# Attention stages of a fused two-block transformer kernel: the value products between a pair's two groups of transposes, the scores of a later pair behind them

## The reference, cut to what matters

```python
s = q @ k.T * scale + bias          # scores
p = exp(s - max(s)); p = p / sum(p) # softmax over the keys
o = p @ v                           # value products
```

## Time and profile before

| what | value |
|---|---|
| median of 3 runs | 3514.08 us |
| lowest, highest | 3511.32, 3519.0 us |
| profiled execution, its own time | 3510.07 us |
| its span | 3508.3 us |
| mean granted TensorE clock | 0.969 of full |
| busy, TensorE matmul | 3260.1 us (93%) |
| busy, VectorE | 2317.3 us (66%) |
| busy, ScalarE | 1332.2 us (38%) |
| busy, GpSimd | 1377.1 us (39%) |

### The profile page before, as it was taken

How to read it: one execution, slowest core, us unless ns; L and a number is a source line. 1 busy time by engine, 2 the same in 40 slices (tenths; PEclk the granted TensorE clock), 3 DMA queues, 4 the chain that set the end, 5 groups by cost and what they waited for, 6 DMA issues and landing times. The chain is left out here.

```text
span 3508.3 us, 51517 instructions
## 1 busy us (share of the span) xinstructions
PE 3260.1 (93%) x18667; PEld 2828.7 (81%) x18667; DVE 2317.3 (66%) x4682; ACT 1332.2 (38%) x2000; POOL 1377.1 (39%) x738
## 2 busy tenths in 40 slices
PE   7878999997999999999898889899989988899998
PEld 5756799997999999999686567788878866668877
DVE  7763989999996888887685667655450067654440
ACT  3344233334554433333312674322231145743331
POOL 3114347765765422222230564222223322444443
PEclk9988999999999999999999999999999999999999
DMA  6412547776999999998355503222212141033322
GB/s 208 153 39 78 186 138 253 233 226 209 365 369 356 359 366 362 367 358 309 126 174 136 92 2 128 82 60 63 62 45 63 47 124 59 33 130 92 94 79 89
DMA packets 235687, 588.98 MB, mean 168 GB/s; under 512 B 52547, under 2 KB 113987, under 8 KB 231404
## 3 DMA queue, kind: packets, MB, share of 16 engines
q1 hardware_dynamic: 177964, 419.63, 36.4%
q0 software_dynamic: 36864, 134.23, 10.5%
q10 hardware_dynamic: 20672, 32.68, 2.6%
HBM read 529.03 MB, written 56.91 MB: 167 GB/s over the span
## 5 line engine op out<-in xcount | busy, mean ns | idle before, releaser
L433 POOL TENSOR_TENSOR ahead_low<-w_raw,ahead_high 128x1024 fp32r<-128x1024 f32 (+1 forms) x159 | 422.0, 2654 | 891.3 <-ACT ahead_high L369 891.3
L230 PE MATMUL psum<-h_low,ahead_high 128*128 128x512 f32 (+1 forms) x1384 | 492.2, 356 | 0.0
L229 PE MATMUL psum<-h_high,ahead_high 128*128 128x512 f32 (+1 forms) x1384 | 491.3, 355 | 0.8 <-POOL ahead_low L433 0.8
L231 PE MATMUL psum<-h_high,ahead_low 128*128 128x512 f32 (+1 forms) x1384 | 489.3, 354 | 0.0
L369 ACT ACTIVATE ahead_high<-w_raw 128x1024 fp32r<-128x1024 f32 (+1 forms) x159 | 178.0, 1119 | 744.3 <-PE psum L231 710.0
L2075 POOL TENSOR_TENSOR pick_u_low<-pick_u_raw,pick_u_high 128x1024 fp32r<-128x1024 f32 x128 | 309.8, 2422 | 191.2 <-ACT pick_u_high L2194 188.9
L229 PE MATMUL psum<-peer_h_high,pick_u_high 128*128 128x384 f32 x1024 | 355.2, 347 | 15.6 <-POOL pick_u_low L2075 15.4
L230 PE MATMUL psum<-peer_h_low,pick_u_high 128*128 128x384 f32 x1024 | 348.4, 340 | 0.0
L231 PE MATMUL psum<-peer_h_high,pick_u_low 128*128 128x384 f32 x1024 | 345.3, 337 | 0.0
L229 PEld LDWEIGHTS psum<-h_high,ahead_high 128*128 128x128 f32 x1384 | 260.3, 188 | 43.3 <-issue 2.4
L231 PEld LDWEIGHTS psum<-h_high,ahead_low 128*128 128x128 f32 x1384 | 260.9, 188 | 38.7
(11 more groups left out here) (435 smaller groups left out, 8175.4 us busy)
## 6 DMA issues: line engine op xcount, KB each, us to landing
pick_u_raw<-in_expert_uT SPq DMA_DIRECT2D x128, 512.0 KB
v_raw<-in_expert_v SPq DMA_DIRECT2D x128, 512.0 KB
mod_w<-in_w_mod SPq DMA_DIRECT2D x88, 512.0 KB, 3.9
w_raw<-in_ffn_up SPq DMA_DIRECT2D x84, 512.0 KB, 3.6
gelu_dram<-pick_gelu ACTq DMA_DIRECT2D x128, 192.0 KB
gates_dram<-gate_plane SPq DMA_DIRECT2D x24, 1024.0 KB
g<-gates_dram SPq DMA_DIRECT2D x31, 768.0 KB
w_raw<-in_ffn_down SPq DMA_DIRECT2D x29, 704.0 KB, 4.1
```

The lines of the kernel that those rows point to most:

```text
L229: nc.tensor.matmul(bank, w_high, x_high, start=first, stop=False)
L230: nc.tensor.matmul(bank, w_high, x_low, start=False, stop=False)
L231: return nc.tensor.matmul(bank, w_low, x_high, start=False, stop=last)
L433: nc.gpsimd.tensor_tensor(w_low[r % 2][:, :, :], raw[r % n_raw][:, :, :], w_high[r % 2][:, :, :].bitcast(F32), ALU.subtract).then_inc(k.w_ ...
```

## The change

The order of the TensorE loop over the pairs is another one. Nothing is added or removed, and no other engine's program changes. For each w: lower transposes of w, value products of w-1, upper transposes of w, scores of w+2.

```diff
             for w in range(n):
                 turn(w, 0)
+                if w:
+                    multiply(w - 1)
+                turn(w, 1)
                 if w + 2 < n:
                     score(w + 2)
-                turn(w, 1)
-                if w:
-                    multiply(w - 1)
             multiply(n - 1)
```

## The result

The changed kernel takes 3629.68 us (median of 4 runs, 3621.64 to 3631.89) beside 3516.54 us of the kernel before on the same chip (4 runs, 3511.32 to 3523.05): a ratio of 1.0319, 95% interval 1.0297 to 1.034. It is 3.2% slower. The forecast was 3621, the range 3572 to 3670.

The account below looks back on a forecast made before the run. A closed loop through TensorE, VectorE and ScalarE was taken to bound the changed kernel. Terms 42.6 (na) + 40.5 (swa) + 11.9 (dil) + 12 (clock) = 107 us gave 3617, put at 3621 us; range 3572 to 3670.

Parts of the forecast that it names:

- The ring: Attention stages: upper transposes, scores, reduction, exponentials, lower copy, next upper transposes; na latent step 5.92 us, was 4.64.
- Na, 42.6 forecast: Stage na: 5.68 us more in each of 8 groups, less 2.85 at the end, 42.6 us added.
- Swa, 40.5 forecast: Stage swa: a step of 5.16 us against 3.81, in 30 steps with scores, 40.5 us added.
- Dil, 11.9 forecast: Stage dil: a step of 3.63 us against 2.78, in 14 steps, 11.9 us added.
- The clock, 12 us taken: All three stages: TensorE's clock falls after idle times; 12 us added, some 13 steps at 0.9.
- the upper end: Rival, clock falls often: 1.6 us lost in two of five of 94 steps, 60 us; 3669 us, chance 0.15.
- The sign of being wrong: Wrong if na's upper transposes stay 4.6 us apart, or if added time lies in steps with clock 0.50.
- The products at nothing: TensorE loop: value products moved ahead of the upper transposes fill the wait for the lower copy; costed at nothing.
- The filled wait: Rival: scores still reduced in time and TensorE loses its waits, 33.7 us gained, 3480 us; chance 0.04.
- The rule that the engine of the highest occupancy comes first: Rival: TensorE's unchanged work bounds the stages, 3514 us, chance 0.02; by the rule at most 33.7 us gain, or nothing.
- The shorter loop: Rival: way from scores to exponential 0.4 us shorter, 94 steps give back 38 us, 3571 us; chance 0.09.
- the loop as summed: Main case: the stages grow by the summed closed loop plus the clock, 3595 to 3645 us; chance 0.70.

Follow-up runs that it names:

- e9: Against the changed kernel: value products of short pairs (one or two tiles) computed four times over; 3611.49 us, 1.028 of the kernel before.
- e3: Against the changed kernel: scores of w+2 moved ahead of the lower transposes of w; 3531.85 us, 1.005 of the kernel before.
- e4: Against the changed kernel: ScalarE runs the exponentials of w+1 between the two copies of w; 3492.7 us, 0.9939 of the kernel before.
- E6: Against the changed kernel: value products of w-1 moved behind the upper transposes, ahead of the scores; 3792.52 us, 1.0794 of the kernel before.
- E2: Against the kernel before: value products of w-1 moved ahead of the upper transposes, scores still ahead of both; 3561.89 us, ratio 1.0136.
- e5: Against the changed kernel: first half of each pair's value products computed twice; 3637.58 us, 1.0356 of the kernel before.

## Why the prediction was right, and where its terms were off

**The ring: right.** Latent step 5.95 (5.92 forecast). The group, from e9, 30.27 (30.60). In swa an undisturbed group of four takes 20.47 us, 5.12 a step (5.16). E3 and e4 open the ring in two ways, at TensorE and at ScalarE, and take most of the loss away (e3, 0.5% left) or all of it (e4): that is shown and not only argued. E6 lengthens it by one part and the step grows by that part.

**Na, 42.6 forecast, 56.6 measured.** The loop was oversized by 0.33 us in 8 groups, 2.6: the two steps with short scores, left at 8.20 together, take 7.74, and the other four are 0.13 longer than summed. Most of the rest is the clock. Against undisturbed steps (5.95, 5.95, 4.08, 3.66, 5.11, 5.51) the steps of the changed kernel are longer by 4.2 us in the first group, 0.6, 0.8, 1.2 and 1.4 in the next four, 3.9, 3.9 and 1.4 in the last three: 17.4 us. Not all of this is the clock. In each of two of the last groups ScalarE runs two pieces of the next stage's weights inside the ring, 0.51 us each (L277; the first at 2153.49, between the exponentials and the lower copy at 2154.01):

```profile
2122.28 0.41 PE L1521 MATMUL psum<-consts,na_scores 128*128 128x128 f32 x2 [2.22 <-ACT na_probsT L1606]
...
2154.52 0.46 PE L1521 MATMUL psum<-consts,na_scores 128*128 128x128 f32 x2 [2.75 <-ACT na_probsT L1606]
```

The second row has the piece ahead of it, the first has not. The prediction's ring has no term for the pieces. They make 2.0 us of the 17.4 and leave 15.4 to the clock; in the kernel before they cost 1.1 (two groups of 25.49 instead of 24.92). The sum 42.6 - 2.6 + 15.4 + 2.0 - 1.1 = 56.3 is the stage to 0.3 us.

**Swa, 40.5 forecast, 37.7 measured.** The step was forecast 0.04 too long, 1.2 us for the 30 steps. With weight pieces and some steps at the lower clock the 30 steps still grew by 41.2 (2935.82 to 3051.65 before, 3018.67 to 3175.70 after). The rest of the stage got 3.5 us shorter, nearly all of it at the end: from those last transposes on the kernel before takes 9.54 us, in part at the lower clock and with one pair's products more still to run, and the changed one 6.53 at a granted 1.00.

**Dil, 11.9 forecast, 18.7 measured.** E9, with the clock at 0.88, has 66.0 us there, 10.1 above before: the loop term was about right, as far as a kernel with another clock than before (0.82) can tell, and the 8.6 us between it and the changed kernel went as the clock rose.

**The clock, 12 us taken, about 24 measured** (15.4 in na, 8.6 in dil, none that can be told from nothing in swa). This is the term that was mis-sized, in the number of steps and in the price of one. Na alone has twelve steps that the clock lengthens, by 1.3 us on the mean; I took some 13 at 0.9 for all three stages. I had put a step's loss at 1.59 us at most, since I let only the transposes and the way to the first reduction hang on the clock; the first step loses 2.03, because VectorE's later reductions wait for the later score matmuls. (The 94 steps of the upper end were miscounted too: 90 have scores, 46, 30 and 14.) I chose the low end "because pairs of rows 3 with their short waits show no fall". Those pairs wait 0.2 to 0.9 us; the rows that had spoken for this case were those of the earlier trace rows, an idle 2.17 us with 0.52 behind it. The changed kernel has idle times of 2.2 us at two places in a group of na, behind the short products of the context pairs, and these I had never looked for: the prediction says "idle times of 1.3 us and more" for all steps alike. The step behind the first of them (5.51 undisturbed) is longer in six of seven groups, up to 7.46 (0.51 of it a weight piece), and the one behind the second (5.95) is 7.4 in four. Shorter waits are not safe by themselves either: in the first group of na, behind one of 1.35 us (1982.05), twelve products at 1985.17 took 2.65 us, and the 6 us from 1982 have 0.72. A list of TensorE's idle time per kind of step, drawn from the same loop, might have come nearer to this term.

The Trainium skill, TensorE: Matmul & The Clock Gate, HAM oscillation — how this bites in real kernels, describes a loop in which the wait in every iteration, there one for DMA of some 3 to 5 us, sends the clock down again. In the changed kernel only the first step of na has a wait of 3 us or more ahead of its transposes (3.25). E6 comes nearest to it, with steps of 9 us again and again; in the changed kernel the trace agrees for part of the groups of na only, and in swa it does not: a wait of 1.31 or 1.67 us stands in every step there, and nearly all but the first and the last steps of the stage keep their length (the last ones are longer by the weight pieces; behind two waits of 2.18 us there, the longest after the start, the clock stays at 1.00).

**Luck in the nearness.** The forecast was 9 us from the median partly because two errors offset each other. Without the clock's 24 us the three stages grew by 89.0, against 95 summed; with the 12 taken for the clock that makes 107 against 113.0. The sign of being wrong that I had named, added time in steps at a clock of 0.50, came true for about a fifth of it.

**The products at nothing: right here, for a reason that is narrower than given.** In the ring they are covered. But they also have a job: they cover the upper copy where they stood before. E2 shows that price, 1.4% or 48 us, where the ring is open. The prediction looked at who waits for the products, and not at what waits behind their absence.

**The rivals.** The filled wait would have paid from a way of 1.1 us between scores and exponential; it is 2.38 (2065.39 to 2067.77). The rule that the engine of the highest occupancy comes first (the Trainium skill, Perfetto Trace Analysis, Identifying the Most-Contended Engine) does not see the ring. (The section itself excepts TensorE, whose busy share of matmuls it calls no good measure of how close the engine is to its roofline; the prediction left that out.) In e5 TensorE had more work and the undisturbed latent steps kept their length, and in e9 it had more work and the kernel took less time. The shorter loop is excluded by 5.95. The time lies in the case of the loop as summed (3595 to 3645).

**Open.** When exactly the clock falls is not settled here: in na it fell behind most of the 2.2 us and some of the 1.35 us and not behind others, and e9 shows it to differ in swa with the same instructions. No kernel with a second set of score banks was run, so that e3's waits come from the single set is read from the code and the waits only. The 8 us outside the stages are within what the other kernels vary there.

## What to carry to other kernels

When engines with orders of their own hand work round, draw the ring: for each instruction that is moved, ask which instruction on the *other* engine next stands in front of what this engine waits for. Position in the loop, not pair number, says when a result is wanted; a result for "two pairs later" may be wanted at once, and moving the consumer by one place (e4) can turn a loss of 3.2% into a gain of 0.6%.

Then count the gaps: with one set of banks that an engine fills and another empties, each fill needs a piece of independent work behind it. Two pieces belong in two gaps. And where a stall is added, list its length per kind of step, since the long ones of na mostly cost twice: the time itself, and the clock behind it. List also what else the engines run inside the ring now and then, here a weight piece of 0.51 us: in na slack hid nearly half of it before, and the closed ring pays it in full.

## What the runs showed of the hardware beyond what was expected

- Work that nobody needs can shorten a stage: 384 more matmul records, na 7.6 us shorter (e9), with the clock at 0.97 instead of 0.92. Spread over all pairs (e5) such work also raised that clock, to 0.96, but lengthened steps without idle time by more than it gave back.
- Idle times of 1.3 to 1.7 us, one in every step of 5 us, left the steps of swa at their length through groups on end, and so did two of 2.18 us, while na, with waits of 1.35 and 2.2 us, lost its clock now and then. The eight score matmuls that come next after 2.2 us of idle time took anything from 1.56 (2122.62) to 2.78 us (2089.70), those after 3.25 us took 2.93.
- The way from the start of the scores to VectorE's first reduction was 0.81 us in every undisturbed pair, before and after, and longer where the clock had fallen: 1.18 us (2089.70 to 2090.88), 1.26 (1969.56 to 1970.82) and 1.34 (2154.91 to 2156.25). The forecast had let this part double at most. What it had left out is the way from there to the exponential, which grew from 1.57 to 2.50 us (1970.82 to 1973.32).
